# Neighbourhood attention in tiles of 8 by 16 queries with per-kind bias tables, and modulation on four column groups

## What is computed

```python
# modulation, layer 0: two rows (latent, context) by 3072 columns
shift, scale, gate = split(silu(c) @ w_ada[l] + b_ada[l], 3)

# neighbourhood attention: 6 heads of 64; a query sees 8 rows by 16 columns of keys
row_start = clip(r - 4, 0, 32 - 8)          # for query row r
col_start = clip(cq - 8, 0, 64 - 16)        # for query column cq
bias = rpb[:, key_row - r + 7, key_col - cq + 15], -inf outside the window
s_loc = (q * 64**-0.5) @ k_window + bias
s_ctx = (q * 64**-0.5) @ k_context          # all 256 context keys
p = softmax(concat([s_loc, s_ctx]));  o = p_loc @ v_window + p_ctx @ v_context
```

## Time and profile before

| | us |
|---|---|
| median of three runs (4531.26 to 4539.04) | 4535.6 |
| the profiled execution | 4525.47 |
| its span in the profile | 4523.4 |
| modulation of layer 0, 9 to 44 of the span | 35 |
| Fourier stage, layer 0 and layer 1 | about 116 and 111 |
| neighbourhood attention, layer 0 and layer 1 | 275 and 259 |

### The profile page before, as it was taken

How to read it: one execution, slowest core, us unless ns; L and a number is a source line. 1 busy time by engine, 2 the same in 40 slices (tenths; PEclk the granted TensorE clock), 3 DMA queues, 4 the chain that set the end, 5 groups by cost and what they waited for, 6 DMA issues and landing times. The chain is left out here.

```text
span 4523.4 us, 68153 instructions
## 1 busy us (share of the span) xinstructions
PE 4104.8 (91%) x26139; PEld 3292.4 (73%) x26139; DVE 2157.1 (48%) x4738; ACT 1489.6 (33%) x3419; POOL 502.3 (11%) x527
## 2 busy tenths in 40 slices
PE   7999999799769899999979957979999979979799
PEld 4777789567558688778857746858778757758687
DVE  5364111267666543111127766732680356657554
ACT  4001443166422220144316622431111357731211
POOL 3021000200010120000020001021340001000100
PEclk9999999899789899999989978989999989989899
DMA  4244221820245532222271034542112133347221
GB/s 187 86 152 139 74 78 60 271 83 14 93 141 213 187 116 72 93 78 79 97 248 54 14 128 162 196 163 83 63 67 85 45 104 112 98 176 265 91 82 63
DMA packets 231158, 521.52 MB, mean 115 GB/s; under 512 B 47002, under 2 KB 101354, under 8 KB 221490
## 3 DMA queue, kind: packets, MB, share of 16 engines
q1 hardware_dynamic: 207220, 436.11, 27.3%
q0 software_dynamic: 23616, 81.06, 4.9%
HBM read 320.66 MB, written 196.43 MB: 114 GB/s over the span
## 5 line engine op out<-in xcount | busy, mean ns | idle before, releaser
L72 PE MATMUL tm_tacc<-tm_tw_hi,hT_hi 128*128 128x384 f32 (+1 forms) x1120 | 413.2, 369 | 19.0 <-DVE tm_tw_lo L897 10.2
L74 PE MATMUL tm_tacc<-tm_tw_hi,hT_lo 128*128 128x384 f32 (+1 forms) x1120 | 409.1, 365 | 0.0
L73 PE MATMUL tm_tacc<-tm_tw_lo,hT_hi 128*128 128x384 f32 (+1 forms) x1120 | 409.1, 365 | 0.0
L72 PE MATMUL tz_tacc<-tz_tw_hi,hT_hi 128*128 128x512 f32 x896 | 359.2, 401 | 5.7 <-POOL tz_tw_lo L926 3.8
L72 PE MATMUL cm_acc<-hT_hi,cm_wb_hi 128*128 128x512 f32 (+1 forms) x912 | 361.8, 397 | 0.0
L73 PE MATMUL tz_tacc<-tz_tw_lo,hT_hi 128*128 128x512 f32 x896 | 355.1, 396 | 0.0
L74 PE MATMUL tz_tacc<-tz_tw_hi,hT_lo 128*128 128x512 f32 x896 | 354.8, 396 | 0.0
L74 PE MATMUL cm_acc<-hT_hi,cm_wb_lo 128*128 128x512 f32 (+1 forms) x912 | 343.6, 377 | 0.0
L73 PE MATMUL cm_acc<-hT_lo,cm_wb_hi 128*128 128x512 f32 (+1 forms) x912 | 343.3, 376 | 0.0
L779 DVE SCALAR_TENSOR_TENSOR tm_ds<-tm_dg,tm_ds 128x512 f32<-128x512 f32 (+1 forms) x40 | 25.6, 639 | 532.1 <-ACT tm_ds L773 532.1
L72 PEld LDWEIGHTS tm_tacc<-tm_tw_hi,hT_hi 128*128 128x128 f32 x1120 | 210.5, 188 | 61.2 <-DVE tm_tw_lo L897 14.3
(11 more groups left out here) (375 smaller groups left out, 8707.2 us busy)
## 6 DMA issues: line engine op xcount, KB each, us to landing
scr_z<-tz_tz SPq DMA_DIRECT2D x112, 256.0 KB
scr_zcm<-cm_zo SPq DMA_DIRECT2D x96, 256.0 KB, 2.0
scr_ztm<-tm_tz SPq DMA_DIRECT2D x68, 256.0 KB, 2.0
scr_xres<-out_x POOLq DMA_DIRECT2D x34, 512.0 KB, 4.0
cm_area<-in_w_ada POOLq DMA_DIRECT2D x64, 256.0 KB, 3.1
scr_z<-out_xn POOLq DMA_DIRECT2D x32, 512.0 KB, 4.8
mo_z<-scr_z SPq DMA_DIRECT2D x16, 1024.0 KB, 5.1
tz_traw<-in_w_in SPq DMA_DIRECT2D x7, 2048.0 KB, 7.8
```

The lines of the kernel that those rows point to most:

```text
L72: nc.tensor.matmul(out, ah, bh, start=start, stop=False)
L73: nc.tensor.matmul(out, ah, bl, start=False, stop=False)
L74: return nc.tensor.matmul(out, al, bh, start=False, stop=stop)
```

## The change

Modulation of layer 0: the stationary operand becomes `cw`, 128 by 32, whose first two columns are the vectors and the others zero. The four products of a block go to the four groups of 32 columns of the array and so to PSUM partitions 0, 32, 64 and 96 of a single bank. One addition of 128 by 512 and four transposes of 128 by 128 replace four additions, one more and 16 small transposes. `b_ada` comes as eight small rows. (The `Modulation` class, which does the gates and layer 1, is unchanged.)

Neighbourhood attention: a tile is 8 rows by 16 columns of queries. A tile's key window is 11 to 16 rows of 31 columns (inner tiles) or 24 (tiles at the left and right edge). Of the 16 tiles four have 496 local keys in 4 blocks of 124, four have 360 in 3 blocks of 120, two have 341, two 372, two 264 and two 288, all in 3 blocks. The keys are read as moving operand in rows of 31 or 24; q is copied and scaled per tile by GpSimd into `qt`; values are loaded per tile into two buffers, one DMA per key block; the output goes to 8 by 16 rows of `mix`. There are nine kinds of tile, each with a bias table of its own; two tables exist at a time. Table 0 is built by VectorE in the Fourier stage, the other eight by GpSimd during the attention, each from `near` (the bias by query and relative position) and a mask: 7 additions of the window's width. `near` comes from 48 skewed reads (16 partitions by 16 pieces of 128 bytes each) instead of 12, six after each of the first eight Fourier stores; the scratch write shrinks from 90 by 64 rows of 512 bytes to 98 by 16 of 192, and six small loads of `lines` are added. The context tiles keep their form.

```diff
@@ ada_phase
-                        last = nc.tensor.matmul(acc[n][0:2, :], cs[:, k, :], wk[k][:, n * 512:(n + 1) * 512],
+                        last = nc.tensor.matmul(acc[32 * n:32 * n + 32, :], cw[:, k, :], wk[k][:, n * 512:(n + 1) * 512],
                                                 start=(k == 0), stop=(k == KC - 1))
-                for j in range(2 * KC):
-                    last = nc.tensor.transpose(tp[:, 2 * j:2 * j + 2], arow[:, j * 128:(j + 1) * 128],
-                                               keep["ident"][0:2, 0:2])
+                for j in range(4):
+                    last = nc.tensor.transpose(tp[:, j * 128:(j + 1) * 128], arow[:, j * 128:(j + 1) * 128], keep["ident"][:, :])
@@ Neighbourhood
+    def load_near(self, eng, io, r):
+        if r == 0:
+            eng.wait_ge(self.pad_out, 16)
+        base = io["rpb_pad"][0, 0, 0:1]
+        for h in range(NA_H):
+            at = base.offset + (7 - r + 15 * h) * QC * 48 + 15
+            src = bass.AP(base.tensor, at, [[47, QC], [QC * 48, 16], [1, 32]])
+            eng.dma_start(self.near[QC * r:QC * (r + 1), h, :, :], src).then_inc(self.near_in, 16)
+    def build(self, eng, y):
...
+        if y >= 2:
+            eng.wait_ge(self.table_ok, y)
+        eng.tensor_tensor(grid(self.mask[:, 0:w.width]), rows[:, :, None].to_broadcast([128, w.nr, w.nc]),
+                          cols[:, None, :].to_broadcast([128, w.nr, w.nc]), ALU.add).then_inc(self.mask_ok, 1)
+        eng.wait_ge(self.mask_ok, y + 1)
+        a, b = w.k0 - w.r0 + 4, w.m0 - w.c0 + 8
+        for h in range(NA_H):
+            last = eng.tensor_tensor(grid(self.table[y % 2][:, h, 512 - w.width:512]), self.near[:, h, a:a + w.nr, b:b + w.nc],
+                                     grid(self.mask[:, 0:w.width]), ALU.add)
+        last.then_inc(self.table_ok, 1)
@@ fourier_phase, SP
-                    if t < 2 * NA_H:
-                        na.load_diagonals(sp, io, t)
+                    if t < QR:
+                        na.load_near(sp, io, t)
@@ fourier_phase, GpSimd
-                na.scale(nc, pool)
@@ neighbourhood_phase, SP
+                def load_v(i):
+                    w = windows[i]
+                    if i >= 2:
+                        sp.wait_ge(pv_mm, NPT * (i - 1))
+                    for j, (r, n, nk) in enumerate(w.chunks()):
+                        src = io["ztm"][0:LX, 1024:1024 + D_NA].rearrange("(r c) d -> r c d", c=GRID)[r:r + n, w.m0:w.m0 + w.nc, :]
+                        sp.dma_start(v[i % 2][0:nk, j, :], src).then_inc(v_in[i % 2], 16)
...
+                    if i + 2 < NWIN:
+                        load_v(i + 2)
@@ neighbourhood_phase, GpSimd (new)
+                def queries(i):
...
+                    if i >= 3:
+                        pool.wait_ge(s_mm, NPT * (i - 2))
...
+                    nc.gpsimd.tensor_scalar(dst, src, NA_D ** -0.5, None, ALU.mult).then_inc(qt_ok, 1)
+                for i in range(len(tiles)):
+                    if i + 2 < len(tiles):
+                        queries(i + 2)
+                    for y in range(1, len(na.kinds)):
+                        if i == first_tile[y - 1]:
+                            if y >= 2:
+                                pool.wait_ge(m_ok, NA_H * i)
+                            na.build(pool, y)
@@ neighbourhood_phase, PE: score_pair
-                    for a, b, k0 in spans:
-                        for h in range(2):
-                            last = nc.tensor.matmul(sp_ps[h][:, a:b], q[64 * h:64 * h + 64, c, tok:tok + 128],
-                                                    kk[64 * h:64 * h + 64, c, k0:k0 + b - a], start=True, stop=True)
+                    for h in range(2):
+                        d = slice(64 * h, 64 * h + 64)
+                        if w:
+                            ks = kk[d, c, 0:LX].rearrange("p (r c) -> p r c", c=GRID)[:, w.k0:w.k0 + w.nr, w.m0:w.m0 + w.nc]
+                            nc.tensor.matmul(sp_ps[h][:, 512 - w.width:512], qt[i % 3][d, c, :], ks, start=True, stop=True)
@@ neighbourhood_phase, DVE: softmax_max
+                        nc.vector.tensor_tensor_reduce(out=ss[:, 0:wl + LC], in0=ps[:, 512 - wl:512 + LC], in1=na.table[y % 2][:, h, 512 - wl:512 + LC],
+                                                       scale=-1.0, scalar=HIGHEST, op0=ALU.add, op1=ALU.min, accum_out=m[:, 1:2]).then_inc(m_ok, 1)
```

More of the change, by code:

```diff
@@ L129, in ada_phase @@
         wk = [P.sb(f"w{k}", [128, 2 * D]) for k in range(KC)]
-        brow = P.sb("brow", [2, 2 * D])
-        arow = P.sb("arow", [2, 2 * D])
+        cw = P.sb("cw", [128, KC, 32])
+        brow = P.sb("brow", [128, 512])
+        arow = P.sb("arow", [128, 512])
         nw = P.sb("nw", [128, KC])
-        acc = [P.ps(f"acc{n}") for n in range(4)]
+        acc = P.ps("acc")
         tp = P.ps("tp")
@@ L962, in _, with __init__, chunks, query_rows @@
                         spatial.act(act, t)
+QR, QC = 8, 16
+PADR = 98
+class KeyWindow:
+    def __init__(self, r0, c0):
+        self.r0, self.c0 = r0, c0
+        rows = range(min(max(r0 - KH // 2, 0), ROWS - KH), min(max(r0 + QR - 1 - KH // 2, 0), ROWS - KH) + KH)
+        self.m0 = min(max(c0 - KW // 2, 0), GRID - 24)
+        self.nc = 31 if 0 < c0 < GRID - QC else 24
+        inner = 0 < r0 < ROWS - QR
+        self.k0, self.nr = rows[0], len(rows)
+        self.step = 5 if inner and self.nc == 24 else 4
+        if inner:
+            self.nr = -(-self.nr // self.step) * self.step
+        self.parts = [min(self.step, self.nr - x) for x in range(0, self.nr, self.step)]
+        self.width = self.nr * self.nc
+        self.kind = (0 if r0 == 0 else 1 if inner else 2, 0 if c0 == 0 else 2 if c0 == GRID - QC else 1)
+    def chunks(self):
+        return [(self.k0 + self.step * j, n, n * self.nc) for j, n in enumerate(self.parts)]
+    def query_rows(self, rows):
+        return rows[0:LX].rearrange("(r c) d -> r c d", c=GRID)[self.r0:self.r0 + QR, self.c0:self.c0 + QC, :]
+def key_windows():
+    all_ = [KeyWindow(r, c) for r in range(0, ROWS, QR) for c in range(0, GRID, QC)]
+    seq = [(1, 1), (1, 0), (1, 2), (0, 1), (2, 1), (0, 0), (0, 2), (2, 0), (2, 2)]
+    return seq, sorted(all_, key=lambda w: seq.index(w.kind))
 class Neighbourhood:
@@ L969, in __init__ @@
         self.last = last
+        self.kinds, self.windows = key_windows()
         self.q = P.sb("q", [128, 3, LX if last else LT])
         self.kk = P.sb("k", [128, 3, LT])
[L973 to L978, removed]
+        self.near = P.sb("near", [128, NA_H, 16, 32])
@@ L1028, in fourier_phase @@
+    def bias(self, nc, dve):
+        nc.vector.memset(self.table[0][:, :, 512:512 + LC], 0.0)
+        dve.wait_ge(self.lines_in, 16 * 6)
+        dve.wait_ge(self.near_in, 16 * NA_H * QR)
+        self.build(dve, 0)
 def fourier_phase(nc, l, io, keep, na):
@@ L1298, in softmax_max @@
                     i, h = units[n]
-                    _, _, nr, b0, inner = tiles[i]
-                    wl = nr * GRID
+                    wl = width(i)
                     dve.wait_ge(s_mm, n // 2 + 1)
@@ L1336, in out @@
                                             rd[:, i % 2, :, None].to_broadcast([128, NA_H, 64]), ALU.mult).then_inc(o_ev, 1)
-                for j in range(2):
-                    last = nc.vector.memset(pt[j][64:128, :, 6, :], 0.0)
-                last.then_inc(pz_ok, 1)
                 nc.vector.memset(pre.ls[:, :], math.log(GDK ** -0.5)).then_inc(pre.ls_ok, 1)
```

207 lines of the change are left out of this document (115 added, 92 removed).

## The result

| | before | changed |
|---|---|---|
| median of the runs, us | 4534.0 (4 runs, 4531.3 to 4539.0) | 4461.7 (4 runs, 4461.1 to 4462.4) |
| the profiled execution and its span | 4525.5, 4523.4 | 4461.45, 4459.6 |

The ratio is 0.9839, with a 95% interval from 0.9822 to 0.9856: 1.6% faster. The gain is 72.3 us where 92.2 were forecast; between the two profiled executions it is only 64.0.

What follows compares the result with a forecast made beforehand. PE's instruction stream was taken to bound the attention, loads the modulation's end, and stores and loads back the Fourier stage. Terms -98.6 + 1.9 - 2.5 + 14.0 - 7.0 = -92.2 took 4535.6 to 4443.4 us, range 4414 to 4482.

Steps and rivals of the forecast that it cites:

- the shared ports: Attention: GpSimd's new work delays VectorE's reduces by 13 us a layer, giving 4470 us; chance 0.12.
- a slow moving operand: Attention scores: keys in rows of 31 or 24 stream slower, some 33 us, giving 4476; chance 0.07.
- The pair of heads: Attention: PE bounds each head pair, and smaller tiles save 49.3 us per layer, 98.6 in all.
- Values per tile ... hidden: Attention: a tile's 0.5 to 0.8 MB of values land within about 5 us, wanted 10 us later, costing nothing.
- The Fourier term: Fourier stage: bias-row reads issued between SP's stores delay the loads back, +9.1 and +4.9 us, +14.0 in all.
- Rival (b): Fourier stage: SP's read issues are cheap, giving 4427 us or a little less; chance 0.15.
- hidden behind their issues: Fourier stage: the short pieces' transfers take at most 3.3 us a step, below SP's 4.1 us of issuing.
- The modulation: Layer 0 modulation: column groups run beside each other and the tail shrinks, ending at 36.3 instead of 43.3 us, -7.0.
- Rival (d): Modulation: the four column groups fail to run beside each other, giving 4448 us; chance counted within the forecast's 0.60.
- Tables on GpSimd, hidden,: Attention: GpSimd's bias-table additions, 5.1 to 9.6 us a table, finish before each table is wanted, costing 0.
- rival (a): Attention: GpSimd's work contends for ports with VectorE's reduces, 13 us a layer, giving 4470 us; chance 0.12.
- Rival (c): Attention scores: moving operand in rows of 31 or 24 keys streams slower, some 33 us, giving 4476; chance 0.07.

Runs made afterwards that it cites:

- experiment 1: Changed kernel with each tile's values asked for ahead of the wait for the output of the tile two before and its store: 4432.8 us.
- experiments 1 to 3: Changed kernel with values asked for earlier, 4432.8 us; value loads of 128 consecutive tokens instead, 4427.3; of as many consecutive tokens as the block has keys, 4463.3.
- experiment 9: Changed kernel with values asked for early, first queries scaled in the Fourier stage, and the 48 bias-row reads issued by GpSimd instead of SP: 4428.2 us.
- experiment 11: Kernel before with the modulation part of the change alone: 4528.4 us against 4531.9, ratio 0.9993.
- experiment 4: Changed kernel with no bias tables built on GpSimd in the attention, every tile using the first kind's table: 4460.9 us.

## Why the prediction came out as it did

The direction, and the range of 4414 to 4482, held; the likeliest value was 18 us too low, and the total hides a larger miss: from profile to profile 92.2 us were forecast and 64.0 measured. That the range held is in part luck. Its upper end was drawn for two rivals that both fell, the shared ports and a slow moving operand, and the 35 us that the values cost instead happened to fit under it.

- **The pair of heads** was right. Its prices of 4.71 and 4.02 us were 4.65 and 3.98, PE stayed the bound, and experiment 1 has the attention at -49.8 us in layer 1 for a forecast of -49.6. In layer 0 it is -53.2, 3.6 more, which I did not follow up.
- **"Values per tile ... hidden"** is the step that failed. It took the landing of one large transfer and scaled it by bytes. The new loads have an outermost dimension of 4 or 5 and run at 100 to 125 GB/s; those of tile 2 landed 11.8 us after the first issue, not 5, against a lead of 9.7. I had priced a failure "in one place" at "some 5 us per layer"; it failed in 17 places, 25.4 us of waits and 9.6 of mostly slower instructions behind them (experiments 1 to 3): 17.5 per layer.
- **The Fourier term, +14.0,** had the right mechanism and too high a price. A read takes 0.49 us from start to start and not 0.62: a step is 3.46 us and not 4.1, eight steps are 5.1 us less per layer, and 9.1 and 4.9 become 4.0 and -0.2; measured +3.7 and +1.2. Rival (b), cheap issues, was half right. The transfers "hidden behind their issues" were not shown to be hidden: with the issues taken off SP's queue the stores still landed late (experiment 9). How much of the 9.6 us per layer is issue and how much transfer stays open.
- **The modulation, -7.0,** was 7.0 at its end. Eight blocks go by at 1.94 us each, at a granted clock of 0.50, and the last ends at 34.0:

```profile
32.06 1.94 PE L176 MATMUL ada_acc<-ada_w,ada_cw 128*32 128x512 f32 x8 [3.08 <-DMA ada_w<-in_w_ada]
...
34.06 0.69 DVE L190 TENSOR_TENSOR ada_arow<-ada_acc,ada_brow 128x512 f32<-128x512 f32 x1
...
34.81 1.11 PE L181 MATMUL ada_tp<-ident,ada_arow 128*128 128x128 f32 x4 [0.81 <-DVE ada_arow L190]
```

  Four groups run beside each other: 0.24 us an instruction at half the clock, where the earlier trace rows have 0.43 at full clock. Rival (d) fell. How much of the 7.0 us is left further on is not told (experiment 11).
- **Tables on GpSimd, hidden,** was right, and rival (a) (4470) fell in experiment 4. The additions take 5.43 / 6 = 0.9 us for 360 elements, within the 2.5 to 3.8 ns. The first `queries` takes 1.17 us, not 0.95. The first scores of the two attention stages wait 14.3 us in all, where they waited 11.2 before: 3.1 more, where 1.9 was forecast.

```profile
904.33 2.34 POOL L1315 TENSOR_SCALAR na_qt<-nain_q 128x384 f32<-128x384 f32 x2 [4.54 <-POOLq L79]
...
909.98 5.43 POOL L1075 TENSOR_TENSOR na_tab<-nain_near,nain_mask 128x360 f32<-128x360 f32 x6
```

- **Rival (c),** rows of 31 or 24 keys as moving operand: 496 and 256 columns of both heads start the transposes 935.94 - 934.47 = 1.47 us after the score, where 768 columns took 1.50. It fell.
- **The rest of the kernel** was taken as constant, and the profiled execution's 10.1 us below the median as a fixed offset. It is not fixed: the changed kernel's profiled execution stands at its median. The code behind the attention of layer 1, the same in all kernels, took 1902.8 us in the profile of before, 1907.9 in that of the changed kernel, and 1901.9 to 1919.5 over all fourteen. The profile of before was its fastest execution of all (others 4526.3 to 4541.6). Adding the whole offset brought the forecast nearer by 10.1 us, by luck.

## What to carry to other kernels

Before a load is called hidden, read its landing from its shape and not from its bytes: look at the outermost dimension on both sides and what divides it (124 consecutive tokens were as slow as 4 rows), and at the rate of a load with the same one. When a transfer is cut into tiles, ask for it at the moment its buffer comes free, in front of any wait on the same queue; here moving two lines was worth 29 us, 40% of the whole change's gain. And when many small transfers stand in a stage's chain, do not count on hiding them by order: five placements here left the stage of layer 0 at 118 to 125 us, and only leaving them out brought it to 108.5. The DMA engines' share of the stage does not tell this in advance: it was 0.80 in the kernel before, 0.66 in the changed kernel and 0.63 without the reads.

## What the runs showed of the hardware

- The rate of a DMA hangs on its outermost dimension and what divides it, not on its bytes: 100 GB/s for 4 and for 124, 125 for 5, about 290 for 120 and 320 for 128, with pieces of 1536 bytes in all of them.
- PE's waits cost more than themselves: 25.4 us of waits in 17 places, 4.3 us at most, went with 8.9 us more of busy time for the same instructions, and the granted clock behind one of 2.05 us was 0.66.
- SP's time to issue a read of 256 pieces is 0.49 to 0.51 us, but 0.81 in a row of 48 right behind 6.9 MB. GpSimd takes 0.55.
- SP issues a load of 4 broken rows in 0.6 to 0.7 us and one of 124 consecutive tokens in some 0.55 (2.22 us for four, 2.67 before).
